# Averages over the model dimension: eight products on TensorE become two, GpSimd adds the rest; the first attention's values come out by channel

## The reference, cut to what matters

```python
p = jax.nn.softmax(jnp.concatenate([s_lat, s_ctx], axis=-1), axis=-1)
o = (jnp.einsum('bhjqk,bjkhd->bjqhd', p[..., :n_lat], v_blk)
     + jnp.einsum('bhjqk,bkhd->bjqhd', p[..., n_lat:], vc))
```

## Time and profile before

| | us |
|---|---|
| median of 3 runs | 3051.2 (3049.75 to 3051.92) |
| the profiled execution | 3050.71 |
| its span, first to last instruction | 3048.9 |
| PE busy | 2942.7 (97%) |
| DVE busy | 1315.5 (43%) |
| ACT busy | 542.1 (18%) |
| POOL busy | 14.0 |
| PE's share of the chain that ended last | 92% |

### The profile page before, as it was taken

How to read it: one execution, slowest core, us unless ns; L and a number is a source line. 1 busy time by engine, 2 the same in 40 slices (tenths; PEclk the granted TensorE clock), 3 DMA queues, 4 the chain that set the end, 5 groups by cost and what they waited for, 6 DMA issues and landing times.

```text
span 3048.9 us, 50476 instructions
## 1 busy us (share of the span) xinstructions
PE 2942.7 (97%) x21420; PEld 1937.8 (64%) x21420; DVE 1315.5 (43%) x3019; ACT 542.1 (18%) x1206; POOL 14.0 (0%) x13
## 2 busy tenths in 40 slices
PE   7999999998999999999899999999999899999998
PEld 4454799983444444567754555544568678877887
DVE  1668888876999887404321111111121432023211
ACT  2214333322211111214300000000011310022000
POOL 0001000000000000000000000000000000000000
PEclk9999999999999999999899999999999999999999
DMA  8241001005676875320299999999962235522451
GB/s 282 91 159 55 1 1 43 1 20 172 216 248 215 261 224 190 124 97 1 114 342 387 379 372 372 374 396 383 378 238 97 83 99 153 148 83 70 152 152 56
DMA packets 351379, 551.01 MB, mean 181 GB/s; under 512 B 14304, under 2 KB 292192, under 8 KB 347840
## 3 DMA queue, kind: packets, MB, share of 16 engines
q1 hardware_dynamic: 351168, 547.89, 51.2%
HBM read 546.80 MB, written 1.05 MB: 180 GB/s over the span
## 4 chain that ended last, share of the span: by engine, by line
PE 92%; DVE 4%; ACT 2%; DMA 1%; issue 0%; SPq 0%; ACTq 0%; DVEq 0%
PE bank L685 16%; PE bank L1374 15%; PE bank L1166 8%; PE bank L1390 8%; PE bank L1567 7%; PE bank L968 7%; PE bank L1180 5%; PE bank L764 3%; PE bank L644 3%; PE bank L1207 2%; PE bank L1111 2%; DVE mix L2155 1%; PE bank L952 1%; PE bank L756 1%; PE bank L1241 1%; PE bank L1322 1%
## 5 line engine op out<-in xcount | busy, mean ns | idle before, releaser
L685 PE MATMUL bank<-a,ring 128*128 128x256 f32 (+1 forms) x1792 | 448.4, 412 | 9.4 <-DVE a L2090 6.6
L2155 DVE SCALAR_TENSOR_TENSOR mix<-arena,csil,mix 128x256 f32<-128x256 f32 x1008 | 402.3, 482 | 30.9 <-ACT mix L1670 30.8
L685 PEld LDWEIGHTS bank<-a,ring 128*128 128x128 f32 x1792 | 339.4, 191 | 115.3 <-issue 62.8
L1374 PE MATMUL bank<-ring,arena 128*32 128x352 f32 x5376 | 402.1, 459 | 1.7 <-DVE small L2694 1.7
L1374 PEld LDWEIGHTS bank<-ring,arena 128*32 128x32 f32 x5376 | 179.7, 110 | 218.9 <-issue 194.9
L1166 PE MATMUL bank<-a,ring 128*128 128x512 f32 x704 | 307.5, 596 | 6.8 <-ACT a L1666 6.8
L1166 PEld LDWEIGHTS bank<-a,ring 128*128 128x128 f32 x704 | 133.2, 191 | 179.7 <-issue 177.8
L1567 PE MATMUL bank<-arena,ring 128*128 128x256 f32 x1024 | 223.5, 379 | 2.0 <-DVE arena L2878 2.0
L1390 PE MATMUL bank<-ring,arena 128*32 128x256 f32 x3840 | 213.3, 379 | 0.0
L1567 PEld LDWEIGHTS bank<-arena,ring 128*128 128x128 f32 x1024 | 194.4, 190 | 29.1 <-DVE arena L2878 2.8
L2761 DVE TENSOR_TENSOR arena<-arena,bank 128x352 f32<-128x352 f32 x48 | 25.0, 521 | 433.7 <-ACT arena L1944 433.7
(11 more groups left out here) (423 smaller groups left out, 3184.0 us busy)
## 6 DMA issues: line engine op xcount, KB each, us to landing
ring<-in_moe_w SPq DMA_DIRECT2D x224, 704.0 KB, 9.2
ring<-in_moe_w SPq DMA_DIRECT2D x160, 512.0 KB, 6.4
ring<-in_mlp_w SPq DMA_DIRECT2D x64, 1024.0 KB, 5.5
arena<-in_ada_w SPq DMA_DIRECT2D x96, 512.0 KB, 3.7
arena<-in_w_ada SPq DMA_DIRECT2D x48, 512.0 KB, 3.6
ring<-in_ffn_w SPq DMA_DIRECT2D x22, 1024.0 KB, 7.9
arena<-in_moe_w SPq DMA_DIRECT2D x32, 704.0 KB, 10.0
h<-in_w_ada SPq DMA_DIRECT2D x8, 2048.0 KB, 7.6
```

The lines of the kernel that those rows point to most:

```text
L685: i = mm(bank[b][:, 0:n], ws[:, k, t * P:t * P + P], rhs[:, k, sl], start=(k == 0), stop=(k == KT - 1))
L1374: i = mm(b[32 * t:32 * t + 32, 0:PART], ac_[:, g, 32 * k:32 * k + 32], by_tile(ws[i_], t), start=(k == 0), stop=(k == KT - 1), skip_group_ ...
L2155: ins = V.scalar_tensor_tensor(dst, x, cond, dst, ALU.mult, ALU.add)
```

## The change

GpSimd gets `sum_of` (below): it adds the first seven tiles of a norm's sum elementwise, six additions one behind the other, each as soon as its tile has arrived. `two_in` then averages on PE the partial sum and the eighth tile. This is done for the squares of stages 1, 2, 3 and 13 (in place, in tile 0 of the squares) and for the means of stages 6, 8, 10 and 12 (in the second half of `tmpB`). For the mean of stage 13 GpSimd adds all eight tiles and PE averages the one sum. In the attention's projection the two averages of stage 13 stand behind the fifth tile, those of stage 3 at the end; DVE's `variance(13)` and `scaled(13)` and ACT's `root(13)` move one tile later.

In the first attention `values` now has 64 channels of v as the stationary operand and the 128 columns of turned weights as the moving one, so that the result lies by channel; head q of the pair goes to partitions 64q to 64q+63. The reciprocals, which lie by token, are spread over the channels by two products with the identity ("r1 spread"), copied by DVE ("r1 out"), and multiplied in. `outputs_turned` and `output_turned` are gone.

```diff
-        otok, o1 = cut(a_t, 0, 2, D), cut(a_t, 2048, KT, TL)
+        rspread, o1 = a_t[:, 0:256], cut(a_t, 2048, KT, TL)
...
+        partial = tmpB[:, TL:T]
+        RESIDUALS = {6: "out2", 8: ("mlp", 0), 10: "fourier", 12: ("mlp", 1)}
...
+            def two_in(name, st, acc, last, b):
+
+                pe.wait_ge(pool_done, at(GP, (name, st)))
+                n = acc.shape[-1]
+                mm(bank[b][:, 0:n], const("mean"), acc, start=True, stop=False)
+                if name == "norm sum":
+                    pe.wait_ge(act_done, at(AC, ("square", st, KT - 1)))
+                else:
+                    pe.wait_ge(vec_done, at(VE, (RESIDUALS[st], KT - 1)))
+                mm(bank[b][:, 0:n], const("mean"), last, start=False, stop=True
+                   ).then_inc(pe_done, did(PE, (name, st)))
+
+            def squares_two(st, sl):
+
+                two_in("norm sum", st, SQUARES[st][:, 0, sl], SQUARES[st][:, KT - 1, sl], SUM_BANK[st])
+
+            def residual_means(st):
+
+                two_in("norm mean", st, partial, hT[:, KT - 1, LAT], 1)
...
                 mix_part(j, (0, 1, 2, 3))
-                if j:
-                    square_in(1, slice(0, T), j - 1)
-            square_in(1, slice(0, T), KT - 1)
+            squares_two(1, slice(0, T))
...
-                if n:
-                    square_in(2, slice(0, T), n - 1)
             sum_up(FT + KT)
             turn_later(FT + KT - 1)
-            square_in(2, slice(0, T), KT - 1)
+            squares_two(2, slice(0, T))
...
             def values(u):
 
                 j, qt = NA_UNITS[u]
+                o = P * (u % 2)
+                pe.wait_ge(vec_done, at(VE, ("r1", u)))
                 if u:
-                    pe.wait_ge(vec_done, at(VE, ("otok", u - 1)))
+                    pe.wait_ge(vec_done, at(VE, ("r1 out", u - 1)))
+                for q in range(2):
+                    i = mm(bank[7][HD * q:HD * q + HD, o:o + P], rsum[:, u, q:q + 1].broadcast_to([P, HD]), ident,
+                           start=True, stop=True, skip_group_check=True)
+                i.then_inc(pe_done, did(PE, ("r1 spread", u)))
                 for q in range(2):
                     pe.wait_ge(act_done, at(AC, ("pt1", u, q)))
-                    hd, o = 2 * j + q, 128 * (u % 2) + 64 * q
-                    for m in range(NCH):
-                        i = mm(bank[6][:, o:o + HD], pt[u % 2][q][:, m, :], v1[:, m, hd * HD:hd * HD + HD],
-                               start=(m == 0), stop=(m == NCH - 1), skip_group_check=True)
-                i.then_inc(pe_done, did(PE, ("o1", u)))
...
                 if u:
                     pe.wait_ge(vec_done, at(VE, ("o1", u - 1)))
+                for m in range(NCH):
+                    for q in range(2):
+                        hd = 2 * j + q
+                        i = mm(bank[6][HD * q:HD * q + HD, o:o + P], v1[:, m, hd * HD:hd * HD + HD],
+                               pt[u % 2][q][:, m, :], start=(m == 0), stop=(m == NCH - 1), skip_group_check=True)
+                i.then_inc(pe_done, did(PE, ("o1", u)))
...
-            pe.wait_ge(ctx2_in, 16)
-            for k in range(KT):
-                add_tile("norm mean", 13, k, hT[:, k, CTX], 2)
+            pe.wait_ge(pool_done, at(GP, ("norm mean", 13)))
+            mm(bank[2][:, 0:TC], const("mean"), tmpB[:, CTX], start=True, stop=True
+               ).then_inc(pe_done, did(PE, ("norm mean", 13)))
 
             def beside(j):
-                square_in(3, LAT, j)
-                if j == 1:
-                    squares_in(13, CTX)
+                if j == 3:
+                    squares_two(13, CTX)
+                if j == KT - 1:
+                    squares_two(3, LAT)
...
                 product(name, s0, 4, rhs, LAT, [2, 3],
-                        lambda j: pe.wait_ge(vec_done, at(VE, (name, j))),
-                        then=lambda j: residual_mean(name, st, j))
+                        lambda j: pe.wait_ge(vec_done, at(VE, (name, j))))
+                residual_means(st)
                 squares_in(st, LAT)
...
-                    if n:
-                        residual_mean(("mlp", i), st + 1, n - 1)
-                residual_mean(("mlp", i), st + 1, KT - 1)
+                residual_means(st + 1)
                 squares_in(st + 1, LAT)
...
+            def sum_of(name, st, dst, tile, arrived, n=KT - 1):
+
+                for k in range(1, n):
+                    if k == 1:
+                        arrived(0)
+                    else:
+                        gp.wait_ge(pool_done, at(GP, (name, st, k - 1)))
+                    arrived(k)
+                    G.tensor_tensor(dst, dst if k > 1 else tile(0), tile(k), ALU.add
+                                    ).then_inc(pool_done, did(GP, (name, st) if k == n - 1 else (name, st, k)))
...
+            sum_of_squares(1, slice(0, T))
+            sum_of_squares(2, slice(0, T))
+            sum_of("norm mean", 13, tmpB[:, CTX], lambda k: hT[:, k, CTX], lambda k: gp.wait_ge(ctx2_in, 16), KT)
+            sum_of_squares(13, CTX)
+            sum_of_squares(3, LAT)
+            for st in (6, 8, 10, 12):
+                sum_of_residuals(st)
...
             def output(u):
 
                 j, qt = NA_UNITS[u]
+                o = P * (u % 2)
+                ve.wait_ge(pe_done, at(PE, ("r1 spread", u)))
+                op(("r1 out", u), V.tensor_copy(rspread[:, o:o + P], bank[7][:, o:o + P]))
                 ve.wait_ge(pe_done, at(PE, ("o1", u)))
...
+                V.tensor_tensor(o1[:, j, qt * P:qt * P + P], bank[6][:, o:o + P], rspread[:, o:o + P], ALU.mult
+                                ).then_inc(vec_done, did(VE, ("o1", u)))
```

More of the change, by code:

```diff
@@ L1537, in _ @@
             pe.wait_ge(vec_done, at(VE, "o_conv"))
-            def residual_mean(name, st, j):
-                pe.wait_ge(vec_done, at(VE, (name, j)))
-                add_tile("norm mean", st, j, hT[:, j, LAT], 1)
             def outwards(name, s0, st, rhs):
                 product(name, s0, 4, rhs, LAT, [2, 3],
-                        lambda j: pe.wait_ge(vec_done, at(VE, (name, j))),
-                        then=lambda j: residual_mean(name, st, j))
+                        lambda j: pe.wait_ge(vec_done, at(VE, (name, j))))
+                residual_means(st)
                 squares_in(st, LAT)
@@ L1913, in _ @@
             for k in range(KT):
-                if k == 4:
+                if k == 5:
                     root(13, CTX)
@@ L2054, in _, with sum_of_squares, sum_of_residuals @@
             G.memset(state, 0.0).then_inc(pool_done, did(GP, "state 0"))
+            def sum_of(name, st, dst, tile, arrived, n=KT - 1):
[7 more added lines that the diff above has]
+                                    ).then_inc(pool_done, did(GP, (name, st) if k == n - 1 else (name, st, k)))
+            def sum_of_squares(st, sl):
+                sum_of("norm sum", st, SQUARES[st][:, 0, sl], lambda k: SQUARES[st][:, k, sl],
+                       lambda k: gp.wait_ge(act_done, at(AC, ("square", st, k))))
+            def sum_of_residuals(st):
+                sum_of("norm mean", st, partial, lambda k: hT[:, k, LAT],
+                       lambda k: gp.wait_ge(vec_done, at(VE, (RESIDUALS[st], k))))
+            sum_of_squares(1, slice(0, T))
[5 more added lines that the diff above has]
+                sum_of_residuals(st)
         @block.vector
@@ L2606, in output @@
                 j, qt = NA_UNITS[u]
+                o = P * (u % 2)
+                ve.wait_ge(pe_done, at(PE, ("r1 spread", u)))
+                op(("r1 out", u), V.tensor_copy(rspread[:, o:o + P], bank[7][:, o:o + P]))
                 ve.wait_ge(pe_done, at(PE, ("o1", u)))
-                V.tensor_tensor(cut(otok[:, qt, :], j * P, 2, HD), cut(bank[6], 128 * (u % 2), 2, HD),
-                                wide(rsum[:, u, :][:, :, None], 2, HD), ALU.mult
-                                ).then_inc(vec_done, did(VE, ("otok", u)))
-            def output_turned(u):
-                j, qt = NA_UNITS[u]
-                ve.wait_ge(pe_done, at(PE, ("o1 turned", u)))
-                V.tensor_copy(o1[:, j, qt * P:qt * P + P], bank[7][:, P * (u % 4):P * (u % 4) + P]
-                              ).then_inc(vec_done, did(VE, ("o1", u)))
+                V.tensor_tensor(o1[:, j, qt * P:qt * P + P], bank[6][:, o:o + P], rspread[:, o:o + P], ALU.mult
+                                ).then_inc(vec_done, did(VE, ("o1", u)))
             n_units = len(NA_UNITS)
@@ L2627, in _ @@
                     output(u - 1)
-                if u >= 2:
-                    output_turned(u - 2)
             output(n_units - 1)
-            output_turned(n_units - 2)
-            output_turned(n_units - 1)
             centre(13, CTX)
@@ L2636, in _ @@
                 residual("na res", j, bank[4 + j % 2][:, 0:TL], (0, 1, 2), (1,))
-                if j == 3:
+                if j == 4:
                     variance(13, CTX)
-                if j == 4:
+                if j == 5:
```

9 lines of the change are left out of this document (removed).

## The result

| | before | after |
|---|---|---|
| median (range) | 3051.56 us (3049.75 to 3052.68) | **3018.39 us** (3017.09 to 3018.65) |
| ratio, 95% interval | | **0.9889** [0.9877, 0.9901] |
| profiled execution, its span | 3050.71, 3048.9 | 3018.25, 3016.4 |

A forecast was written before the change was run, and what follows sets the result against it. The prediction took PE (busy 97%) as the bound; 0 + 5.1 + 6.2 + 2.2 + 3.0 + 5.1 + 10.3 = 31.9 off the profiled 3050.71 gave 3018.8, median 0.5 above: 3019.3 us. Range 3014 to 3030.

The forecast's parts named there:

- Price of a product on PE: Each averaging product taken off PE saves 0.86 us at 512 columns, 0.43 at 256; six count per sum.
- Norm 1: Sum after the mixer: 2.6 us gained before residual 4, 2.6 lost to POOL's adds slowing DVE; net 0.
- everything goes by DVE's 7.72: Norm 1: from residual 4 on, DVE sets the pace, with residuals 7.72 us apart.
- the fourth rival: Attention: waits of PE drop its clock to half; all 15 units slower, 3069 us; chance 0.03.
- Norm 2: Sum after the feed-forward: six products off PE gain 5.1 us, since DVE has 7.72 of slack.
- The second rival: Norm 2's gain is eaten by POOL's hold on DVE, norm 1 loses 2 more; 3026 us; chance 0.1.
- Attention: First attention, steady units: column halves overlap, a unit takes 3.52 us, not 3.93; 0.41 x 15 = 6.2 gained.
- the ring: Attention: scores, maxima, exponentials, ACT's copy, transposes to later scores; 7.04 us for two units, 3.52 each, against PE's 3.41.
- End of the attention, mean 13, projection, four means: Four separate terms, from the attention's end to the late norms' means: gains of 2.2, 3.0, 5.1 and 10.3 us.
- Rival 1: Attention: the column halves don't overlap, PE takes 4.4 us per unit; 3034 us; chance 0.1.
- rival 3: Late layers: weight loads set the pace, so the four means' 10.3 us is lost; 3030 us; chance 0.04.
- rival 5: PE still waits for partial sums, seven ends each late by an add of 1 us; 3026 us; chance 0.03.

The follow-up runs named there:

- experiment 5: The changed kernel with the means of norms 6, 8, 10 and 12 averaged tile by tile on PE again; 3026.75 us.
- experiment 9: The changed kernel with the squares of norms 3 and 13, in the attention's projection, summed singly on PE again; 3023.72 us.
- experiment 2: The changed kernel with the squares of norm 2 back on PE; 3024.92 us.
- experiment 1: The changed kernel with the squares of norm 1 back on PE; 3017.26 us.
- Experiment 6: The changed kernel, but in norm 1 POOL adds only tiles 0 to 3 and PE averages the squares of tiles 4 to 7 singly; 3014.66 us.
- experiment 7: The changed kernel, but in the attention ScalarE copies a unit's turned weights before the next unit's exponentials; 3013.35 us.
- experiment 4: The changed kernel with the attention's value products ordered as all of head 0, then all of head 1; 3023.59 us.
- experiment 10: The changed kernel with the attention's value products in pairs, two of head 0, then two of head 1, and so on; 3017.17 us.
- experiment 8: The changed kernel with the edits of experiment 6 and experiment 7 together; 3012.98 us.
- experiment 11: The program of experiment 8 run once more, unchanged; 3012.39 us.

## Why the prediction was right

The number and the sign held, and so did the account of who bounds each stage. Luck helped in two terms, norm 1 and the attention, which were right as sums and not in all their parts, and 1.4 behind the attention's projection was in no term. Point by point:

- **Price of a product on PE** (0.86 and 0.43, six per sum). Held to 0.1 us in every sum but norm 1's, and in the stages that experiments 5 and 9 undo, up to the last residual (to 0.4 in experiment 2). Where the total moved by another amount (experiment 5: 8.4 for 10.35) the difference is a change of granted clock elsewhere.
- **Norm 1: 0.** The result held (experiment 1), the working only in its main part. Forecast were 2.6 won before residual 4 and 0.85 lost per tile to POOL's hold; measured were 2.6 and 0.58 from residual to residual, so 0.87 was left at residual 7. What took that was not in the sum: PE emptied for 5 us, and its last product ran at half clock. These are two misses of opposite sign, so that the term came out at 0 was luck. Behind the forecast's step "everything goes by DVE's 7.72" a look at what PE does in the meantime was missing; the fourth rival asked the same question for the attention, where the clock stayed at 1.00. Experiment 6 shows what was to be had: 2.6.
- **Norm 2: 5.1.** Held (5.1), by the slack that the forecast named: the earlier trace rows 7.72, now 6.16. The second rival fell.
- **Attention.** The 6.0 against 6.2 is partly luck: the forecast multiplied the saving of a steady unit, 0.41, by 15, but only 12 intervals are steady (0.40 each) and the third saves 0.5, together 5.2; the other 0.8 was the dip of the clock in the kernel before. The prediction saw that dip and put no term for its going. Forecast 3.52 per unit by the ring and 3.41 by PE; measured 3.53 and, in experiment 7, 3.32. The ring's sum of two units was right to 0.03; that it shows as one unit at PE's pace and one that waits was not forecast. PE's part was put 0.09 too high: the value and spread instructions start 0.054 apart and not 0.056, and a change of form takes 0.17, not 0.19. The choice that carried the term, full overlap of the column halves by the quarters' row, is borne out. The Trainium skill ("TensorE: Matmul & The Clock Gate", "Measured speedup vs the span model") gives 2.38x for three column tiles. The prediction's estimate by it, 1.35 for 20 instructions and 3.63 for a unit, is a little off: 2.16 / (2 x 0.79) is 1.36, the unit 3.65, the term 4.2 and not 4.5. This trace doesn't agree with it: the 20 instructions take 1.08, 0.054 each. The Trainium skill says on the same page, under "What overlaps and what doesn't", that weight loads overlap running products only where the row group differs. For these halves, which share their rows, that doesn't hold (0.054 against 0.108 per instruction, both in experiment 4's trace).
- **End of the attention, mean 13, projection, four means:** 2.2, 3.0, 5.2, 10.35, each within 0.1.
- **What wasn't in the sum:** the start shifted by +1.0 in code that nothing touched. And 1.7 came in ahead of the experts, where the kernel before ran at a granted clock of 0.50 from 1505 to 1525 and the changed one mostly higher; 1.4 of it goes with the projection's sums (experiment 9), in code that the edit doesn't touch. Together with the 0.8 in the attention these partly cancelled. Shifts of 1 to 3 us in untouched code set how well any forecast of this kernel can do.

Rival 1 (no overlap) would have needed units of 4.4; rival 3 late weights; rival 4 a clock below 1.00 in the attention; rival 5 POOL in the chain. The changed kernel's trace has none of them.

## What to carry to other kernels

Moving sums off the bounding engine pays its price per instruction where that engine is late, and nothing where another one is: read for each place who waits for whom before and after, and move only the tiles ahead of the point at which the bound changes (here tiles 0 to 3 of norm 1). Where the engine that is relieved then stands idle for microseconds ahead of a short last step, that step may run at half clock and eat what was won. And when a ring through another engine becomes the bound, look first at the order within that engine's queue: here two lines moved on ScalarE gave 3.9, about half of the 7.4 that the rebuilt attention had given. And before a stage's gain is credited to an edit, compare the granted clock there in both traces: 0.8 of this attention's 6.0 was clock.

## What the runs showed of the hardware that was not expected

- **Products of the other column half pass those in front of them**, by three instructions in both orders that were tried (experiments 4 and 10). With eight and eight the first of head 1 starts 0.44 after head 0's first in place of 0.86. The Trainium skill ("TensorE: Matmul & The Clock Gate", "What overlaps and what doesn't") has products start in strict program order. These starts don't agree. Only starts are meant: ends are modelled in the trace.
- **A GpSimd add beside VectorE's products costs them 0.71**, not its own 1.27 (512 columns), in the mixer and in the feed-forward alike. It starts 0.35 ahead of them, and the first product alone is longer. Forecast was 0.85.
- **The same code ran the same 16 instructions in 3.72 or in 5.41** (granted clock 1.00 or 0.75, for norm 8's squares) in different kernels and in different executions of one (norm 10's squares in experiments 8 and 11, which are one program: 3.72 and 5.41). Whether a norm's short sum behind an idle stretch is caught by the lower clock depends on things that the edits don't touch. It moved the total by 1.7 at a time, and the lower clock of experiment 8's first trace by about 3, which is why stages, and not totals, decide in the experiments above.
